# Prompt attention groups combined block by block during the gate projection, on GpSimd, in a hybrid decoder layer

## The chip, the cores and the metric

The kernel runs on one core of one Trainium2 chip. The metric is the device time of one execution in microseconds (us). The engines are TensorE (PE; its weight loads stand in the trace as PEld), VectorE (DVE), ScalarE (ACT), GpSimd (POOL) and SyncE (SP), which here only issues DMAs. A row of the trace gives the start in us from the beginning of the profiled span, the duration in us, the engine, the line of the kernel, the operation and its tiles.

## The reference, cut to what matters

One decoder layer for 1024 prompt tokens and 8 x 8 new tokens ("samples") that share the weights: a half SwiGLU step, a mixer with two branches (an mLSTM and a dilated attention with three head groups), and another half SwiGLU step. What the change touches is the end of the attention branch. Each of the three groups g leaves for each token and head an output and a log of its softmax denominator, and the groups are merged with these as weights:

```
wts = jax.nn.softmax(jnp.stack(lses), axis=0)
y_a = jnp.einsum('gbsh,gbshd->bshd', wts, jnp.stack(outs)).reshape(B, S, A_OUT_WIDTH)
y_a = y_a @ w_up_a
merged = jax.nn.sigmoid(gm) * y_m + jax.nn.sigmoid(ga) * y_a
x = x + merged @ w_out
```

The sample rows attend to cached keys and values (8 sequences with 1152 kept keys each) and to their 8 new keys and values.

## The kernel before, in words

Weights stream as slabs of 128 x 2048 floats (1 MB). Each slab lands in `raw`, and POOL splits it into a high and a low part, one instruction each (`ring_split`, L737 and L739); PE makes three products per tile from the parts. Three slabs are in flight; a slab may be split once PE has released a place.

After the first SwiGLU and the q, k, v projections comes the **slot stage**. Slot n (0 to 83) is half of a projection unit on PE (`pair_unit`, 24 matmuls) followed by a piece of other work (`mixture_slot`). Slots 3 to 39 do prompt attention; each of its 35 units stores unnormalised outputs, their sum and the negated maximum to the DRAM tensor `o_att` (token, group, head, 66 floats). From slot 44 on the mLSTM runs in ten slots for each of four heads (`lstm_slot`, position i = 0 to 9): at slot 44 + 10h + i PE turns and scores chunk i (`keys_and_scores`, L958, L959), DVE scales (L1995), updates the state and the hidden rows. At i = 6 DVE prepares the decay of the next head (`args`, L1958 to L1967), at i = 7 the samples' values (`sample_parts`), at i = 1 it needs a square root from ACT for the previous head (L1530, L2052, L2053). Slots 36 to 83 project the two branch gates, which ACT evacuates with a sigmoid in each odd slot (L1471). Slots 84 to 90 finish the last head without projections.

Then comes the **tail**, in which nothing is projected. SP loads the cached keys `kc` (8 loads) and values `vc` (8 loads); half of them, for pass 0, are issued at slot 82 (`SLOTS - 2`) and behind slot 83. Pass B (B = 0, 1; four sequences each) is: `s_scores` (L1129, L1135 cached keys, L1142 new keys), `s_max` on DVE (L2160), `s_exps` on ACT (L1610), `s_turn` on PE (L1154), a copy on DVE (L2171), `s_values` on PE (L1165, L1167), `s_outputs`, `s_out_turn` (L1174) and `s_out` (L2184), which leaves `soT`. The wait before L1142 is for the semaphore `s_new`, which counts the new keys `sks` and the new values `vnw` together.

Interleaved with the two passes, eight blocks of 128 tokens are combined: SP loads `oc` from `o_att` (two buffers), DVE forms the weights' exponents (L2194 to L2196), ACT takes the exponential (L1616), DVE multiplies and adds (L2203 to L2207), divides (L2209, L2212) into `yat`, PE turns it (`c_turn`, L1183), DVE copies it out (L2220) and SP stores it to `mix[4:6]`. On PE the order is fixed by hand: scores 0, turn of block 0, `s_turn(0)`, block 1, values 0, block 2, `s_out_turn(0)`, blocks 3 to 5, scores 1, turn, values 1, block 6, out turn 1, block 7.

After both, the **merge stage** multiplies the branches with `w_up` (L774 to L776 on `mx_hi`, `mx_lo`), gates them with `sgate` (L2262) and goes on to `w_out`. It needs the inputs `mxin` (six loads from `mix` for each chunk of 384 tokens), the three slabs from `S_UP` on, and the samples' rows stored from `soT`.

Of the kernel before, what the change touches and what calls it, by code (L numbers as in the profile page):

```python
# [116 lines left out]
S_NEW = 16 * (8 + G)  # L117
# [7 lines left out]
HEAD_SLOTS = 10  # L125
SLOTS_END = LSTM_SLOT + HEAD_SLOTS * H + 7
# [3 lines left out]
def program(nc, stream, xT, cols, masks, amasks, cos_t, sin_t, state_in, m_in, kc_in, vc_in,  # L130
# [14 lines left out]
    with ctx:  # L145
# [99 lines left out]
        put = overlay(TEMP + 6144)  # L245
        sqj = put("sqj", [P, DK])
# [38 lines left out]
        ocw = put("ocw", [P, 2, G, H])  # L285
        ocm = put("ocm", [P, 2, H])
# [7 lines left out]
        put = overlay(TEMP + 6656)  # L294
        smk = put("smk", [SROW, KEYS_S])
        put = overlay(TEMP + 6656)
        sqs = put("sqs", [P, G, 2, SAMP])
        yat = put("yat", [P, 2, H * HD])
        yT = put("yT", [P, 2, 2, P])
        put = overlay(ACTS)  # L300
        oc = put("oc", [P, 2, G, H, HD + 2])
        oacc = put("oacc", [P, 2, H, HD + 1])
# [24 lines left out]
        c_in = [sem(f"c_in{i}") for i in range(2)]  # L327
        mix_stored = [sem(f"mix_stored{i}") for i in range(2)]
# [58 lines left out]
        oc_read = sem("oc_read")  # L387
        oce_ready = sem("oce_ready")
# [12 lines left out]
        s_queries = sem("s_queries")  # L401
        s_new = sem("s_new")
# [46 lines left out]
        def _(sp):  # L449
# [119 lines left out]
            def slot(m):  # L569
# [62 lines left out]
            load_heads(sks, kr_out, s_new)  # L632
# [10 lines left out]
            for n in range(2):  # L643
                sp.dma_start(oc[:, n], o_att[n * P:(n + 1) * P]).then_inc(c_in[n], 16)
# [17 lines left out]
            def combined(n):  # L662
                if n + 2 < NBLK:
                    sp.wait_ge(oc_read, n + 1)
                    sp.dma_start(oc[:, n % 2], o_att[(n + 2) * P:(n + 3) * P]).then_inc(c_in[n % 2], 16)
                sp.wait_ge(yT_ready, n + 1)
# [8 lines left out]
            for n in range(2, 5):  # L675
                combined(n)
# [1749 lines left out]
```

## Time and profile before

| | us |
|---|---|
| three timed runs | 2746.63, 2737.41, 2746.70 |
| median | 2746.63 |
| profiled execution, device time | 2736.92 |
| its span | 2734.7 |
| PE busy in the span | 2581.5 (94%) |
| DVE, POOL, ACT busy | 975.4, 816.9, 431.1 |

The profiled execution is a run of its own, near the fastest of the three. PE is busy nearly everywhere; in the page's 40 slices of 68 us the PE digits are 9 except at the start and in slices 24 to 28 (`3 7 8 9 8`), which hold the end of the slot stage, the tail and the merge stage.

### The profile page before, as it was taken

Reading aid. Unit: us, or ns where it says so; the run is one execution under the profiler, and the core shown is the slowest. Engines: PE = TensorE matmul, PEld = TensorE weight load, DVE = VectorE, ACT = ScalarE, POOL = GpSimd, SP = SyncE. Lnnn points to the kernel's source line nnn. Section 1 sums busy time; section 2 is a strip of 40 time slices with the busy share of each in tenths; the row PEclk is TensorE's granted clock in tenths of the full one; section 3 lists DMA queues with packets and bytes.
Section 4 is the critical chain, followed back from the end, with each engine's and each line's share of the span. In section 5 each row is a group of like instructions: output and inputs, shape, how many; then the busy total and the mean of one; then the engine's idle time right before and its main releaser. Section 6 shows DMA issues by size and latency. Waiting matters only on the chain. (4 is left out here: it accounts for less than half of the span.)

```text
span 2734.7 us, 39075 instructions
## 1 busy us (share of the span) xinstructions
PE 2581.5 (94%) x16101; PEld 2513.9 (92%) x16101; DVE 975.4 (36%) x1969; ACT 431.1 (16%) x934; POOL 816.9 (30%) x202
## 2 busy tenths in 40 slices
PE   7999999999998999999999963789899999999997
PEld 6999999999997999989999951789899999999997
DVE  5322222222256134322244335545522222222226
ACT  4100000000031000133433320112200000000003
POOL 3333333333322423322132103041333333333330
PEclk9999999999999999999999986889999999999999
DMA  4110111111102524514333275440111111111101
GB/s 151 56 46 32 46 46 46 46 46 46 46 16 85 175 73 123 140 58 123 109 138 131 101 277 228 150 137 16 45 56 38 46 46 46 46 46 46 37 10 66
DMA packets 102912, 219.72 MB, mean 80 GB/s; under 512 B 30788, under 2 KB 81404, under 8 KB 87836
## 3 DMA queue, kind: packets, MB, share of 16 engines
q1 hardware_dynamic: 61544, 188.80, 20.0%
q10 hardware_dynamic: 41268, 29.50, 3.4%
q8 instruction: 73, 1.20, 0.2%
q14 instruction: 27, 0.22, 0.0%
HBM read 172.38 MB, written 45.89 MB: 80 GB/s over the span
## 5 line engine op out<-in xcount | busy, mean ns | idle before, releaser
L822 PE MATMUL ps<-h_hi,whi 128*128 128x384 f32 (+1 forms) x3072 | 1017.0, 331 | 11.8 <-DVE h_lo L1709 11.8
L823 PE MATMUL ps<-h_lo,whi 128*128 128x384 f32 (+1 forms) x3072 | 1007.5, 328 | 0.0
L824 PE MATMUL ps<-h_hi,wlo 128*128 128x384 f32 (+1 forms) x3072 | 1007.4, 328 | 0.0
L737 POOL TENSOR_TENSOR whi<-raw,con 128x2048 fp32r<-128x2048 f32 x98 | 353.8, 3610 | 1841.9 <-PEq L805 1548.7
L822 PEld LDWEIGHTS ps<-h_hi,whi 128*128 128x128 f32 x3072 | 578.9, 188 | 16.6 <-issue 10.5
L823 PEld LDWEIGHTS ps<-h_lo,whi 128*128 128x128 f32 x3072 | 579.0, 188 | 0.7 <-issue 0.2
L824 PEld LDWEIGHTS ps<-h_hi,wlo 128*128 128x128 f32 x3072 | 578.5, 188 | 0.0
L739 POOL TENSOR_TENSOR wlo<-raw,whi 128x2048 fp32r<-128x2048 f32 x98 | 454.6, 4639 | 7.7
L774 PE MATMUL ps<-act_hi,whi 128*128 128x384 f32 (+1 forms) x1056 | 346.1, 328 | 9.8 <-DVE x L1729 7.7
L1738 DVE TENSOR_TENSOR ps<-silu,ps 128x384 f32<-128x384 f32 x132 | 71.3, 540 | 793.1 <-PE ps L824 555.3
L1729 DVE SCALAR_TENSOR_TENSOR x<-ps,x 128x384 f32<-128x384 f32 (+1 forms) x528 | 281.8, 535 | 201.0 <-PE ps L776 199.5
L776 PE MATMUL ps<-act_hi,wlo 128*128 128x384 f32 (+1 forms) x1056 | 345.5, 327 | 0.0
L775 PE MATMUL ps<-act_lo,whi 128*128 128x384 f32 (+1 forms) x1056 | 345.4, 327 | 0.0
L1300 ACT ACTIVATE silu<-ps 128x384 f32<-128x384 f32 x132 | 62.4, 473 | 1250.5 <-PE ps L824 1250.4
L774 PEld LDWEIGHTS ps<-act_hi,whi 128*128 128x128 f32 x1056 | 198.3, 188 | 12.1 <-DVE x L1729 8.8
L775 PEld LDWEIGHTS ps<-act_lo,whi 128*128 128x128 f32 x1056 | 198.4, 188 | 0.0
L776 PEld LDWEIGHTS ps<-act_hi,wlo 128*128 128x128 f32 x1056 | 198.3, 188 | 0.0
L774 PE MATMUL ps<-whi,h_hi 128*128 128x256 f32 x360 | 103.3, 287 | 7.8 <-DVE h_lo L1709 7.6
L775 PE MATMUL ps<-wlo,h_hi 128*128 128x256 f32 x360 | 102.5, 285 | 0.0
L776 PE MATMUL ps<-whi,h_lo 128*128 128x256 f32 x360 | 102.0, 283 | 0.0
L1740 DVE TENSOR_TENSOR act_lo<-ps,act_hi 128x384 fp32r<-128x384 f32 x132 | 70.7, 536 | 71.2 <-ACT act_hi L1302 71.2
L774 PEld LDWEIGHTS ps<-whi,h_hi 128*128 128x128 f32 x360 | 69.4, 193 | 9.2 <-DVE h_lo L1709 9.2
(226 smaller groups left out, 2094.6 us busy)
## 6 DMA issues: line engine op xcount, KB each, us to landing
raw<-stream SPq DMA_DIRECT2D x99, 1024.0 KB, 4.8
vc<-vc_in SPq DMA_DIRECT2D x8, 1170.0 KB, 11.1
kc<-kc_in SPq DMA_DIRECT2D x8, 1152.0 KB, 9.5
zgate<-stage ACTq DMA_DIRECT2D x16, 384.0 KB, 2.4
sgate<-zgate SPq DMA_DIRECT2D x16, 384.0 KB, 3.3
zqko<-stage ACTq DMA_DIRECT2D x12, 384.0 KB, 2.7
oc<-o_att SPq DMA_DIRECT2D x8, 396.0 KB, 3.9
va_out<-sva ACTq DMA_DIRECT2D x24, 130.0 KB, 1.8
```

The costliest lines, as they stand in the source:

```text
L737: pool.tensor_tensor(hi, raw[:, j, :], con[:, C_ONES:C_ONES + 1].to_broadcast([P, SLAB]), ALU.mult).then_inc(hi_split, 1)
L739: pool.tensor_tensor(lo, raw[:, j, :], hi.bitcast(F32), ALU.subtract).then_inc(slab_ready, 1)
L774: pe.matmul(out, w_hi, x_hi, start=(k == 0), stop=False)
L775: pe.matmul(out, w_hi, x_lo, start=False, stop=False)
L776: last = pe.matmul(out, w_lo, x_hi, start=False, stop=(k == nk - 1))
L822: pe.matmul(out, w_hi, h_hi[:, k, a:a + w], start=(k == 0), stop=False)
L823: pe.matmul(out, w_hi, h_lo[:, k, a:a + w], start=False, stop=False)
L824: mm = pe.matmul(out, w_lo, h_hi[:, k, a:a + w], start=False, stop=(k == KT - 1))
L1300: act.activation(silu[:, par, 0:w], bank(2 * par, w), ACT.Silu).then_inc(silu_done, 1)
L1729: dve.scalar_tensor_tensor(x[:, d, a:a + w], bank(4 + v % ACC, w), 0.5, x[:, d, a:a + w], ALU.mult, ALU.add).then_inc(acc_free, 1)
L1738: dve.tensor_tensor(up, silu[:, par, 0:w], up, ALU.mult).then_inc(mul_done, 1)
L1740: dve.tensor_tensor(act_lo[:, j, a:a + w], up, act_hi[:, j, a:a + w].bitcast(F32), ALU.subtract).then_inc(pair_free, 1)
```

## The change

It moves the combination of the prompt's groups out of the tail into slots 43 to 81, one block every five slots, and takes its products and sums from DVE to POOL. There is one buffer each for `oc`, `yat` and `yT`, and they lie where nothing else is live in those slots. The turn of block n on PE stands in slot `COMBINE_AT[n]` = 46, 51, 56, ..., 81, ahead of that slot's `L958`; the next slot waits for its copy (`yT_ready`). `ring_split` of the last five slabs of the stage is written out by hand on POOL between the blocks. The mask `smk` is loaded at slot 82 and no longer at slot 60, and DVE's `sample_mask` moves from slot 81 to 82. `s_new` is parted: `s_keys` for the new keys, `s_new` for the values, waited for in `s_values`. In the tail, SP loads the merge stage's first four inputs early and the slabs `S_UP + 3` to `+ 5` behind inputs 4 and 5.

```diff
+COMBINE_AT = [LSTM_SLOT + 2 + 5 * n for n in range(NBLK)]
@@ SP, slot(m)
-                if m == 60:
+                if m == COMBINE_AT[0] - 3:
                     for s in range(2):
                         sp.wait_ge(o_stored[s], 16 * len(UNITS[s::2]))
-                    sp.dma_start(smk[:], amasks[0:SROW, A_SAMP:A_N]).then_inc(s_mask, 16)
+                    load_block(0)
+                if m - 1 in COMBINE_AT:
+                    n = COMBINE_AT.index(m - 1)
+                    if n + 1 < NBLK:
+                        sp.wait_ge(ya_ready, n + 1)
+                        load_block(n + 1)
+                    sp.wait_ge(yT_ready, n + 1)
+                    sp.dma_start(mix[4:6, :, n * P:(n + 1) * P].rearrange("j p t -> p j t"), yT[:]).then_inc(mix_stored, 16)
                 if m >= LSTM_SLOT:
                     lstm_slot(m - LSTM_SLOT)
                 if m == SLOTS - 2:
                     sp.wait_ge(head_done, TURNS * (H - 1))
+                    sp.dma_start(smk[:], amasks[0:SROW, A_SAMP:A_N]).then_inc(s_mask, 16)
                     sp.wait_ge(slab_ready, S_UP)
                     load_keys_s(0)
                     load_keys_s(1)
+                    load_heads(sqs, qr, s_queries)
+                    sp.wait_ge(smb_ready, 1)
                     load_values_s(3)
-                    sp.wait_ge(smb_ready, 1)
-                    load_heads(sqs, qr, s_queries)
...
+            sp.wait_ge(mix_stored, 16 * NBLK)
+            for k in range(4):
+                load_branch(0, k)
             sp.wait_ge(sv_full, 1)
             for b in range(GROUP, NB):
                 load_values_s(b)
...
+            load_branch(0, 4)
+            load_branch(0, 5)
             for s in range(S_UP + 3, S_UP + 6):
                 slab_behind(s, s % 3)
@@ POOL
+            def combine(n):
+                pool.wait_ge(oce_ready, n + 1)
+                for g in range(G):
+                    last = pool.tensor_tensor(oc[:, g, :, 0:HD + 1], oc[:, g, :, 0:HD + 1],
+                                              ocw[:, g, :].unsqueeze(2).to_broadcast([P, H, HD + 1]), ALU.mult)
+                last.then_inc(oc_ready, 1)
+                pool.wait_ge(oc_ready, 3 * n + 1)
+                for g in range(1, G):
+                    pool.tensor_tensor(oc[:, 0, :, 0:HD + 1], oc[:, 0, :, 0:HD + 1], oc[:, g, :, 0:HD + 1],
+                                       ALU.add).then_inc(oc_ready, 1)
+                    pool.wait_ge(oc_ready, 3 * n + 1 + g)
+                pool.wait_ge(oc_read, n + 1)
+                if n > 0:
+                    pool.wait_ge(yt_full, n)
+                pool.tensor_tensor(yat[:], oc[:, 0, :, 0:HD], ocm[:].unsqueeze(2).to_broadcast([P, H, HD]),
+                                   ALU.mult).then_inc(ya_ready, 1)
...
+            mixed = (S_F + 6 + 9) // 3
+            order = [(6 * (s - S_F - 6) - 7, s, None) for s in range(3 * mixed, S_UP)]
+            order += [(COMBINE_AT[n] - 1.5, None, n) for n in range(NBLK)]
+            for _, s, n in sorted(order, key=lambda e: e[0]):
+                if n is None:
+                    ring_split(s // 3, s % 3)
+                else:
+                    combine(n)
@@ PE, keys_and_scores
+                m = LSTM_SLOT + HEAD_SLOTS * h + c
+                if m in COMBINE_AT:
+                    c_turn(COMBINE_AT.index(m))
+                elif m - 1 in COMBINE_AT:
+                    pe.wait_ge(yT_ready, COMBINE_AT.index(m - 1) + 1)
@@ PE, tail
-                pe.wait_ge(s_new, S_NEW)
+                pe.wait_ge(s_keys, S_KEYS)
...
-            s_scores(0)
-            c_turn(0)
-            s_turn(0)
-            c_turn(1)
...
+            for B in range(PASSES):
+                s_scores(B)
+                s_turn(B)
+                s_values(B)
+                s_out_turn(B)
@@ ACT, mixture_slot(n)
+                for at_ in (n + 1, n + 2):
+                    if n % 2 == 0 and at_ in COMBINE_AT:
+                        group_exps(COMBINE_AT.index(at_))
@@ DVE
+            def group_weights(n):
+                dve.wait_ge(c_in, 16 * (n + 1))
...
+            def group_sums(n):
+                dve.wait_ge(oc_ready, 3 * n + 3)
+                dve.reciprocal(ocm[:], oc[:, 0, :, HD]).then_inc(oc_read, 1)
...
+                if n in COMBINE_AT:
+                    c_out(COMBINE_AT.index(n))
+                if n + 3 in COMBINE_AT:
+                    group_weights(COMBINE_AT.index(n + 3))
+                if n + 1 in COMBINE_AT:
+                    group_sums(COMBINE_AT.index(n + 1))
-                if n == SLOTS - 3:
+                if n == SLOTS - 2:
                     sample_mask()
```

## Rows read from the trace of the kernel before

**Rows 1.** Waits by pair: in all, times, longest; turns of blocks in the tail.
```profile
PE ps L1183 <- DVE yat L2212: 50.6, 8, 15.8
```
**Rows 2.** Timeline of the tail: start, us, engine, line, tiles, [idle before <- releaser].
```profile
1633.54 0.43 DVE L2206 TENSOR_TENSOR oacc<-oc 128x260 f32<-128x260 f32 x1
...
1641.61 3.71 DVE L2206 TENSOR_TENSOR oacc<-oc 128x260 f32<-128x260 f32 x1
1645.11 4.56 POOL L739 TENSOR_TENSOR wlo<-raw,whi 128x2048 fp32r<-128x2048 f32 x1
...
1653.75 0.69 PE L1183 MATMUL ps<-con,yat 128*128 128x128 f32 x2 [15.76 <-DVE yat L2212]
```
**Rows 3.** Timeline of the tail: both passes' scores, pass 1 to its end.
```profile
1628.10 0.83 PE L1142 MATMUL ps<-sks,sqb 128*32 128x8 f32 x48 [5.09 <-DMA vnw<-va_out]
...
1686.71 5.63 PE L1135 MATMUL ps<-kc,sqb 128*32 128x128 f32 x48
...
1699.80 5.98 PE L1165 MATMUL ps<-vc,spt 128*32 128x260 f32 x72 [1.76 <-DVE spt L2173]
...
1712.36 0.28 DVE L2184 COPY soT<-ps 64x128 f32<-64x128 f32 x1 [0.57 <-PE ps L1174]
```
**Rows 4.** Timeline of DVE: the merge stage's first gating.
```profile
1726.52 0.56 DVE L2262 TENSOR_TENSOR mgt<-ps,sgate 128x384 f32<-128x384 f32 x1 [4.57 <-PE ps L776]
```
**Rows 5.** Timeline of SP's queue: DMA issues, from slot 82 to the end of the tail.
```profile
1589.36 1.28 SPq L604 DMA_DIRECT2D kc<-kc_in  x2
...
1626.92 0.83 SPq L644 DMA_DIRECT2D oc<-o_att  x2
...
1686.59 3.07 SPq L451 DMA_DIRECT2D raw<-stream  x3
```
**Rows 6.** Two stretches: length, busy time (count) of PE, PEld, DVE, ACT, POOL; clock; DMA share; GB/s.
```profile
1590.00:1626.00 36.00, 26.50 (x163) 17.58 (x161) 13.21 (x46) 9.43 (x26) 0.00 (x0) 0.80 0.98 359
1630.00:1650.00 20.00, 2.82 (x12) 2.34 (x12) 15.59 (x26) 1.85 (x5) 8.69 (x3) 0.59 1.01 416
```
**Rows 7.** The tile kc: its loads' time to landing.
```profile
DMA to landing us min/median/max: 6.0/9.5/20.1
```
**Rows 8.** Timeline of slots 43 to 45: SP's queue, PE and DVE.
```profile
1389.68 1.22 SPq L451 DMA_DIRECT2D raw<-stream  x2
...
1395.64 0.27 PE L958 MATMUL ps<-con,kT 128*128 128x128 f32 x1
...
1392.02 0.29 DVE L1995 TENSOR_TENSOR Pm<-ps,Wd 128x128 f32<-128x128 f32 x1 [4.56 <-ACT Wd L1503]
```
**Rows 9.** The tile raw, 1380 to 1402: its three loads' time to landing.
```profile
DMA to landing us min/median/max: 5.0/10.1/12.1
```
**Rows 10.** Timelines of slots 51, 52: a split on POOL, the decay on DVE, the next L958.
```profile
1425.94 6.50 POOL L739 TENSOR_TENSOR wlo<-raw,whi 128x2048 fp32r<-128x2048 f32 x1
...
1427.90 4.63 DVE L1967 SCALAR_TENSOR_TENSOR Wd<-Wd,gcol,msk 64x64 f32<-64x64 f32 x1
...
1432.88 0.27 PE L958 MATMUL ps<-con,kT 128*64 128x128 f32 x1 [2.97 <-DVE Pm L1995]
```
**Rows 11.** Timelines of ACT, DVE and PE, slots 55 and 56 (i = 1, 2).
```profile
1453.93 1.28 ACT L1530 ACT_TABLE_LOAD   x1
1455.22 0.30 ACT L1530 ACTIVATE var<-var,con 128x9 f32<-128x9 f32 x1
...
1455.81 0.17 DVE L2053 TENSOR_TENSOR scl<-var,rden 128x9 f32<-128x9 f32 x1
...
1457.37 0.27 PE L958 MATMUL ps<-con,kT 128*128 128x128 f32 x1
```
**Rows 12.** Timelines of DVE and PE: the end of slot 60's decay, and slot 61; slot 81.
```profile
1483.64 0.28 DVE L1967 SCALAR_TENSOR_TENSOR Wd<-Wd,gcol,msk 64x64 f32<-64x64 f32 x1
...
1484.02 0.27 PE L958 MATMUL ps<-con,kT 128*128 128x128 f32 x1
...
1594.04 1.65 DVE L1984 TENSOR_SCALAR vex<-v,own 64x129 f32<-64x129 f32 x8
```

More of the change, by code:

```diff
@@ L116 @@
 S_QUERIES = 16 * 8
-S_NEW = 16 * (8 + G)
+S_KEYS = 16 * 8
+S_NEW = 16 * G
 ATT_IN = (16 * 8, 16 * 8, 16 * 16)
@@ L245, in program @@
         put = overlay(TEMP + 6144)
+        oc = put("oc", [P, G, H, HD + 2])
+        yat = put("yat", [P, H, HD])
+        yT = put("yT", [P, 2, P])
+        ocw = put("ocw", [P, G, H])
+        ocm = put("ocm", [P, H])
+        put = overlay(TEMP + 11904)
         sqj = put("sqj", [P, DK])
@@ L293, in program @@
         so = put("so", [P, 2, H, HD])
-        put = overlay(TEMP + 6656)
+        put = overlay(X_HI)
         smk = put("smk", [SROW, KEYS_S])
-        put = overlay(TEMP + 6656)
+        put = overlay(TEMP + 8192)
         sqs = put("sqs", [P, G, 2, SAMP])
[L298 to L302, printed above, removed]
         put = overlay(ACTS)
@@ L326, in program @@
         blk_ready = sem("blk_ready")
-        c_in = [sem(f"c_in{i}") for i in range(2)]
-        mix_stored = [sem(f"mix_stored{i}") for i in range(2)]
+        c_in = sem("c_in")
+        mix_stored = sem("mix_stored")
         con_in = sem("con_in")
@@ L749, in _ @@
             ring_split(0, 2)
-            with pool.Fori(1, S_OUT // 3 + 1) as i:
+            mixed = (S_F + 6 + 9) // 3
+            with pool.Fori(1, mixed) as i:
                 for j in range(3):
                     ring_split(i, j)
+            order = [(6 * (s - S_F - 6) - 7, s, None) for s in range(3 * mixed, S_UP)]
[5 more added lines that the diff above has]
+                    combine(n)
+            for s in range(S_UP, S_OUT + 1):
+                ring_split(s // 3, s % 3)
             ring_split(S_OUT // 3 + 1, 0)
@@ L946, in where, with c_turn @@
                 return n, slice(c * P, c * P + n)
+            def c_turn(n):
+                pe.wait_ge(ya_ready, n + 1)
+                if n > 0:
+                    pe.wait_ge(yT_ready, n)
+                for i in range(2):
+                    mm = pe.transpose(ps[:, 5, 256 + i * P:256 + (i + 1) * P],
+                                      yat[:, 2 * i:2 * i + 2, :].rearrange("p h e -> p (h e)"), ident)
+                mm.then_inc(yt_full, 1)
             def keys_and_scores(h, c):
@@ L1175, in s_out_turn @@
                 mm.then_inc(sot_full, 1)
-            def c_turn(n):
-                pe.wait_ge(ya_ready, n + 1)
-                if n >= 1:
-                    pe.wait_ge(yT_ready, n)
-                for i in range(2):
-                    mm = pe.transpose(ps[:, 7, i * P:(i + 1) * P], yat[:, n % 2, i * P:(i + 1) * P], ident)
-                mm.then_inc(yt_full, 1)
-            s_scores(0)
-            c_turn(0)
-            s_turn(0)
-            c_turn(1)
-            s_values(0)
-            c_turn(2)
-            s_out_turn(0)
-            for n in range(3, 6):
-                c_turn(n)
-            s_scores(1)
-            s_turn(1)
-            s_values(1)
-            c_turn(6)
-            s_out_turn(1)
-            c_turn(7)
+            for B in range(PASSES):
[3 more added lines that the diff above has]
+                s_out_turn(B)
             pe.wait_ge(slab_ready, S_UP + 3)
@@ L1495, in att_copy, with group_exps @@
                 act.activation(apt[u % 2][:], ps[:, 6, :], ACT.Copy).then_inc(pt_ready, 1)
+            def group_exps(n):
+                act.wait_ge(ocw_ready, n + 1)
+                act.activation(ocw[:], ocw[:], ACT.Exp).then_inc(oce_ready, 1)
             def exps(h):
@@ L1612, in s_exps @@
                 ins.then_inc(sp_ready, 1)
-            def group_exps(n):
-                act.wait_ge(ocw_ready, n + 1)
-                act.activation(ocw[:, n % 2], ocw[:, n % 2], ACT.Exp).then_inc(oce_ready, 1)
             s_exps(0)
-            for n in range(6):
-                group_exps(n)
             s_exps(1)
-            for n in range(6, NBLK):
-                group_exps(n)
-            act.wait_ge(ya_ready, NBLK)
             for k in range(6):
@@ L2232, in _ @@
             s_outputs(0)
-            block(2)
             s_out(0)
-            for n in range(3, 6):
-                block(n)
             s_max(1)
@@ L2239, in _ @@
             s_outputs(1)
-            block(6)
             s_out(1)
-            block(7)
             def branch_low(c, k):
```

86 lines of the change are left out of this document (20 added, 66 removed).

## The prediction

> **What bounds the kernel now.** I read the page's 40 slices first: PE is the engine that is always busy, but for slices 24 to 28. Then the waits by pair: in the tail PE waits 50.6 us, eight times, for `yat` [rows 1], the block that DVE has just combined and that PE's fixed order wants turned before it goes on. The timeline of the tail shows the worst one, 15.76 us, with `s_values(0)` standing behind it [rows 2]. Its cause is in the same rows: the sum of 0.43 us takes 3.71 us when POOL is splitting a slab, and ends when POOL's instruction does. So from about 1616 to 1722 PE is not the bound; a chain is (scores, maxima, exponentials, turn, values, and eight blocks in between), ending with `soT` at 1712.64 [rows 3] and the first gating of the merge stage at 1726.52 [rows 4]. Whatever shortens the chain shortens the kernel one for one, until a transfer ends later. Before slot 84 it is the other way round: PE is the bound, DVE has 3 to 4 us free in each slot of about 5.3 us, and what is added there costs only where PE comes to wait. The sum is therefore tail gain minus slot stalls, against the profiled execution's 2736.92 us. That one lies 9.7 under the median of the timed runs, 2746.63; with it, two of four runs lie near 2737 and two near 2747, so I count the result from their middle, 2742.
>
> **The tail, part by part.**
> 1. Scores 0 no longer wait for the values: 5.09 us [rows 3]. The new keys are issued ahead of three 1.2 MB value loads and the `vnw` loads behind them, so I take them as landed. Scores 0 end at 1628.93 - 5.1 = 1623.8.
> 2. Pass 0 without blocks. Pass 1 gives the durations: from the first key matmul to `s_values` 1699.80 - 1686.71 = 13.1 us [rows 3], and from there 5.98 + about 0.6 for the new values, 0.7 for DVE's division, 1.1 for the out turn, 0.3 for the copy: 8.9 us. So 22.0 us from first key matmul to `soT`. Pass 0 would be over near 1640, and pass 1 could start there instead of at 1686.71.
> 3. It can't, since now transfers end last. The DMA engines are full from 1590 to 1626 (share 0.98) and again from 1630 to 1650 (1.01, 416 GB/s) [rows 6]. Keys 6 and 7 are issued behind `sample_scored`, and the slowest key load takes 20.1 us [rows 7], so they land near 1652. What changes for them: three `oc` loads of 0.4 MB go from in front of them [rows 5], 1.2 MB / 0.416 = 2.9 us less. But SP now reaches slot 82's loads later. It must first store block 7, which DVE copies behind `sample_parts` of slot 81, over at 1595.7 [rows 12], plus 0.6: SP goes on at 1596.5, and issues the first keys near 1597 and not at 1589.36 [rows 5]. 7.7 us of full rate are lost, of which the dips of the first stretch (359 against 416 [rows 6]: 36 x 57 / 416 = 4.9 us) can give back up to 4.9; bounds 2.8 to 7.7, I take 4.5. The store of head 3 lands behind this backlog, and keys 4 and 5 wait for it as the `oc` loads do at 1626.92 [rows 5]: 1631.4. From there 7.9 MB (four key loads, three slabs) at 0.41 MB per us are 19.2 us, with a little of the merge inputs: pass 1 starts at 1651.5, and `soT` would come at 1673.5. The four values (4.8 MB, with 0.8 MB merge inputs) land by about 1665, wanted at 1664.6: 0.5 more. `soT` at 1674.
> 4. Slabs 59 to 61 are split on POOL in 3 x 8.4 = 25 us from about 1643, ready at 1668: covered by the chain by 6 us. If they landed 12 us later they would be the bound.
> 5. From `soT` to the first gating: before 1726.52 - 1712.64 = 13.9 us, two blocks' work among them. Now SP has behind `soT` inputs 4 and 5 (which wait for DVE's `mx_lo`, 1.1 us), then three slabs of 1 MB that before were issued at 1686.59 [rows 5], then the four `soT` stores, and `sgate` behind their landing. 3.1 MB at 0.416 take 7.6 us, and the stores land behind them: 1.7 + 7.6 + about 0.7 + 3.2 for `sgate` = 13.2 us. The blocks' time is given back to the slabs. Bounds: 8 (stores not held by slabs) to 16.
> Gain of the tail: 1712.64 - 1674 + 0.7 = **39.3 us**. With pass 1 at 1640 in place of 1651.5 (point 3) it would be 51.
>
> **The slot stage, part by part.**
> 1. Block 0. DVE's `group_weights(0)` stands in slot 43 and waits for a load that SP issues right behind slab 55, at 1390.2 [rows 8]. That slab lands 10.1 us after 1389.7 [rows 9], so `oc` at about 1400.3, where DVE was ready at 1387.5 (its next instruction idled 4.56 us [rows 8]). Queued behind the wait on ACT are `group_exps(0)` and the exponentials of head 0's decay, and behind those on DVE the masked scores of slot 44, at 1392.02 before [rows 8]. They come at about 1402.7; PE wants them at 1395.64 [rows 8]: 7.0 us. Bounds: 1 (landing in 4) to 9.5 (12.1).
> 2. POOL's instructions. No row has a small one. 2048 elements take 4.56 us [rows 2], 2.23 ns each, so 260 take 0.58 if the time goes by the elements. The bounds are DVE's 0.43 and, if it were all fixed cost, the split's 4.56 [rows 2]; I take 0.58, since the instruction on DVE shrinks in this way too, and leave the far end to rival C. The first five of a block run a slot ahead, hidden; the last (`yat`) is on the path: DVE's reciprocal, product, three handovers, 1.1 us from DVE's last instruction before it to PE.
> 3. Slots at i = 7 behind a decay (51, 61, 71). At slot 61 the decay ends at 1483.92 and PE wants L958 at 1484.02 [rows 12]: 1.0 us. The other two by like rows 0.9 and 1.6: 3.5.
> 4. Slots at i = 2 behind a head's square root (56, 66, 76). The exponential of the block needs another table on ACT, and the sigmoid's back again, ahead of the root: 1.28 us per load [rows 11]. DVE's `scl` ends at 1455.98, plus 1.28 + 1.1, against L958 at 1457.37 [rows 11]: 1.0. The others by like rows 1.0 and 1.7: 3.7.
> 5. POOL and DVE in each other's way. In slot 51 the split and the decay collide: 4.63 us for an instruction of 0.28, and PE waits 2.97 [rows 10]. After the change POOL holds that split back until block 1 is over, so this collision goes, but the split then falls on `sample_parts` and the copy of the turned block, for which slot 52 now waits. I count this place as even, and the same at slots 71 and 72 (new) as 1.5; bounds 0 to 4 each.
> 6. Sixteen turns on PE: 0.3 us per block beside 0.69 in the tail [rows 2]: 2.4.
> Sum: 7.0 + 3.5 + 3.7 + 1.5 + 2.4 = **18.1 us**. `s_scores` start, mask (0.15 MB, DVE idle in slot 83) and the 16 extra table loads in other slots are covered by 3 us of idle time per slot; if that cover is gone, each table load is 1.3 us.
>
> The collision is what the Trainium skill describes (SBUF: State Buffer, on the port pair shared by DVE and GpSimd): an exclusive lock, the later one blocks fully. By that rule the trace agrees, and every new POOL product is a chance of a block. For a table switch the skill (ScalarE: Activation LUTs, What ACT_TABLE_LOAD costs) gives 1283 ns plus a drain of 1380 ns; the next instruction here starts at 1455.22, 1.29 after the load began [rows 11], so no drain is seen; with it, three i = 2 slots would cost an estimated 4 us more.
>
> **The rivals.**
> A. *Covered slots.* Block 0's load is early, and DVE's and POOL's lateness is absorbed: slots cost 5. 39.3 - 5 = 34 us gained, 2708. For it: 3 us idle per slot; against: the order behind slab 55.
> B. *The tail is held by transfers longer.* The backlog of slot 82 costs its full 7.7, pass 1's values land 5 late, and slabs sit in front of the stores for 16: 39.3 - 3.2 - 5 - 2.8 = 28, minus 18.1: 10 gained, 2732. For it: share 1.01.
> C. *Slower: the blocks' handover chain stalls every slot.* Each block goes DVE, ACT, POOL, DVE, POOL, PE, DVE, PE. If locks, a fixed cost of POOL's products and table loads make PE wait more than 39.3 / 8 = 4.9 us per block, the kernel is slower; at 6.5 us per block, 52 - 39.3 = 13 lost, 2755. Against: only one lock of over 3 us reaches PE in the slots before (2.97).
> D. *The change doesn't do what it says:* the new keys land no earlier than the values did. Then 5.1 of the gain is nothing on PE; as transfers bound pass 1, the time moves by 1 at most: 2722. It is within the forecast.
> By the skill (GPSIMD Engine Reference, Engine selection) two-input elementwise work is about twice as slow on GpSimd. That rule holds for the work moved, and its time is off the path but for `yat`; by it `yat` would take an estimated 0.9 us, 2 us more in all, no other result.
>
> **How the numbers follow.** Forecast: 39.3 - 18.1 = 21.2 us gained, 2742 - 21 = 2721 us (2715.7 against the profiled execution), chance 0.52 with D, own range 2708 to 2732. A 0.18, B 0.19, C 0.11. The range takes in A with its lower level of run (2737 - 37 = 2700) and B with the upper (2747 - 7 = 2740). Half a per cent, 13.7 us, is about what a measurement tells from no change. Faster by more: the forecast but for its weak end, and A: 0.72. Within: B mostly: 0.19. Slower: 0.09.
>
> **What would show it.** Right: PE's wait at slot 45 of about 7 us for `Pm`; waits of 1 to 2 us ahead of `L958` or the turn at slots 51, 56, 61, 66, 71, 76; first `kc` load near slot 82's L958; in the tail a PE wait for DMA `kc` of about 10 us ahead of pass 1's L1135, no waits for `yat`; `soT` 39 us nearer to the first `L1129`-run's start than the old 97 us; first `sgate` landing 13 us behind `soT`. Wrong: a POOL product of over 1 us (the reading by elements falls), or a wait at the merge stage's start for slab 61.

## The result, and the profile after

| | before | after |
|---|---|---|
| timed runs, median (lowest to highest) | 2745.57 us (2737.41 to 2747.55), 6 runs | 2725.47 us (2725.15 to 2727.34), 6 runs |
| profiled execution: its time, and its span | 2736.92, 2734.7 | 2727.34, 2725.3 |
| slot 44's key turn to slot 82's, on PE | 205.5 us | 233.0 us |
| slot 82's key turn to the end of `soT` | 116.1 us | 80.3 us |
| end of `soT` to the first gating on DVE | 13.9 us | 17.5 us |

The ratio is 0.9945, 95% interval 0.9928 to 0.9961: faster, by 11 to 20 us. The forecast was 2721 us, the range 2700 to 2740. The two profiled executions differ by less, 9.6 us; the section on the prediction comes back to this. One of the four timed runs of e10 below was a slow one, at 5112.67 us, and is left out of its median.

A slot's key turn is its L958, the turn of its keys. The lines have moved: L958 is now L997, L1135 is L1174, L1165 is L1205, L2184 is L2231, L1984 is L2002, and POOL's split L737 and L739 is L732 and L734. First the page of after, its slices (each a fortieth of the span, busy tenths):

```profile
PE   7999999999997999999988895789999999999997
DVE  5322222222246134422225431546522222222226
PEclk9999999999998999999999996889999999999999
DMA  3111111111102523524333338540011111111101
```

Counted from 0, slices 23 to 28 of PE's row were `6 3 7 8 9 8` before and are `9 5 7 8 9 9` now: the hole is shallower and begins later, and it is still there. New are the three digits 8 in slices 20 to 22 (1363 to 1567 us, in the slot stage), which were 9. PE's waits by pair (in all, times, longest) say what is in it and what came new:

```profile
PE ps L1174 <- DMA kc<-kc_in: 11.4, 2, 10.1
PE ps L997 <- DVE yT L2126: 9.1, 2, 4.9
PE ps L997 <- ACT kw L1539: 7.6, 1, 7.6
PE ps L978 <- POOL yat L756: 5.9, 6, 1.5
```

The 50.6 us for combined blocks in the tail [rows 1] have gone. In their place stand 11.4 us for keys from DMA (tail) and 22.6 us in three new groups of the slot stage: for the copy of a turned block, for block 0's exponentials (`kw` on ACT) and for POOL's product `yat`. The timeline of the tail, which answers to [rows 3] and [rows 4], PE and then DVE:

```profile
1662.60 6.38 PE L1205 MATMUL ps<-vc,spt 128*32 128x260 f32 x72 [1.76 <-DVE spt L2220]
...
1681.66 5.31 PE L1174 MATMUL ps<-kc,sqb 128*32 128x128 f32 x48 [10.06 <-DMA kc<-kc_in]
...
1696.40 6.54 PE L1205 MATMUL ps<-vc,spt 128*32 128x260 f32 x72 [3.43 <-issue]
...
1709.99 0.66 PE L798 MATMUL ps<-mx_hi,whi 128*128 128x384 f32 x1 [5.02 <-DVE mx_lo L2248]
```
```profile
1705.01 0.28 DVE L2231 COPY soT<-ps 64x128 f32<-64x128 f32 x1 [0.74 <-PE ps L1214]
...
1722.78 0.56 DVE L2261 TENSOR_TENSOR mgt<-ps,sgate 128x384 f32<-128x384 f32 x1 [13.04 <-DMA sgate<-zgate]
```

The two longest waits of this tail are for transfers: pass 1 waits 10.06 us for its keys, and the first gating 13.04 us for `sgate`. SP's queue shows why. It answers to [rows 5]:

```profile
1624.57 0.37 SPq L601 DMA_DIRECT2D mix<-yT  x1
...
1625.49 0.90 SPq L619 DMA_DIRECT2D kc<-kc_in  x2
...
1660.55 0.83 SPq L619 DMA_DIRECT2D kc<-kc_in  x2
...
1706.63 1.38 SPq L455 DMA_DIRECT2D raw<-stream  x3
1708.06 3.43 SPq L687 DMA_DIRECT2D mix<-soT  x4
1719.45 4.74 SPq L698 DMA_DIRECT2D sgate<-zgate  x3
```

Block 7's store stands ahead of the first keys, keys 4 and 5 come 35 us behind these, and the 3 MB of slabs go out 1.4 us ahead of the `soT` stores, whose landing `sgate` awaits: 11.4 us from the first store's issue to the first `sgate`.

In the slot stage the rows of block 0 are these, on DVE and on PE, at slot 45. SP issued the load at 1391.31, and DVE could start on it 10.4 us later:

```profile
1401.73 0.17 DVE L2109 TENSOR_TENSOR ocm<-oc 128x4 f32<-128x4 f32 x1 [13.23 <-DMA oc<-o_att]
...
1404.39 0.45 PE L997 MATMUL ps<-con,kT 128*128 128x128 f32 x1 [7.56 <-ACT kw L1539]
```

And these are slots 51 and 52, POOL, DVE and PE, which answer to [rows 10]:

```profile
1435.63 0.61 POOL L756 TENSOR_TENSOR yat<-oc,ocm 128x256 f32<-128x256 f32 x1 [3.38 <-issue]
1436.20 3.60 POOL L732 TENSOR_TENSOR whi<-raw,con 128x2048 fp32r<-128x2048 f32 x1
1439.88 4.54 POOL L734 TENSOR_TENSOR wlo<-raw,whi 128x2048 fp32r<-128x2048 f32 x1
```
```profile
1435.33 0.17 DVE L2119 RECIPROCAL ocm<-oc 128x4 f32<-128x4 f32 x1
...
1438.54 1.28 DVE L2000 TENSOR_SCALAR own<-msk,wsc 64x8 f32<-64x8 f32 x1
1439.86 6.01 DVE L2002 TENSOR_SCALAR vex<-v,own 64x129 f32<-64x129 f32 x8
1445.79 0.41 DVE L2126 COPY yT<-ps 128x256 f32<-128x256 f32 x1
```
```profile
1436.49 0.41 PE L978 MATMUL ps<-con,yat 128*128 128x128 f32 x2 [0.63 <-POOL yat L756]
...
1446.34 0.40 PE L997 MATMUL ps<-con,kT 128*64 128x128 f32 x1 [4.91 <-DVE yT L2126]
```

The eight products of L2002 take 1.65 us where they are alone [rows 12, the same instructions before]; here they take 6.01. The longest of them takes 4.64 us, about as long as POOL's split beside it, which ends at 1439.88 + 4.54 = 1444.42; the other seven follow at 0.27 each. The copy of the turned block stands behind them on DVE, and PE, which the program lets go on only behind this copy (`yT_ready`), stands 4.91 us.

### The profile page after: what moved, and what is told of

It reads as the page before. It is cut to its first block and busy times, and to the rows that moved or that the text cites. A ratio compares the mean times of both kernels' runs of the same rounds, so it can differ in the third digit from the quotient of the medians.

```text
span 2725.3 us, 39068 instructions
## 1 busy us (share of the span) xinstructions
PE 2580.9 (95%) x16101; PEld 2513.9 (92%) x16101; DVE 944.7 (35%) x1921; ACT 448.4 (16%) x948; POOL 845.4 (31%) x250
## 5 line engine op out<-in xcount | busy, mean ns | idle before, releaser
L848 PE MATMUL ps<-h_hi,wlo 128*128 128x384 f32 (+1 forms) x3072 | 1008.3, 328 | 0.0
L732 POOL TENSOR_TENSOR whi<-raw,con 128x2048 fp32r<-128x2048 f32 x98 | 353.5, 3608 | 1637.4 <-PEq L829 1436.7
L734 POOL TENSOR_TENSOR wlo<-raw,whi 128x2048 fp32r<-128x2048 f32 x98 | 452.5, 4618 | 7.7
```

What stands on the lines that cost most here:

```text
L732: pool.tensor_tensor(hi, raw[:, j, :], con[:, C_ONES:C_ONES + 1].to_broadcast([P, SLAB]), ALU.mult).then_inc(hi_split, 1)
L734: pool.tensor_tensor(lo, raw[:, j, :], hi.bitcast(F32), ALU.subtract).then_inc(slab_ready, 1)
L848: mm = pe.matmul(out, w_lo, h_hi[:, k, a:a + w], start=False, stop=(k == KT - 1))
```

## The experiments

All are timed beside the kernel before, whose median lay between 2736.4 and 2742.9 us in these comparisons. They were made at four later times, on different chips (e1 to e4, e5 to e8, e9 and e10, e11), and after was not timed again in them. So a difference between two medians of the table can hold a few us that are not the edit's. By their ratios to before, e3 and e6 (0.9945 and 0.995) can't be told from after (0.9945), and the intervals of e1 (0.9896 to 0.9944), e2 (0.9906 to 0.9945) and e4 (0.9864 to 0.9938) overlap that of after; e5 (0.9978 to 1.0007) and e8 (0.9803 to 0.9853) lie clear of it. What each single edit did is therefore read from its trace. To place a gain I use PE's key turns of slots 44 and 82, the end of `soT` and the first product of the merge stage, in each run's trace:

| run | median us | slots 44 to 82 | slot 82 to start of `soT`'s last copy | slot 82 to merge stage | merge stage to end |
|---|---|---|---|---|---|
| before | 2745.57 | 205.5 | 115.8 | 125.7 | 1012.5 |
| after | 2725.47 | 233.0 | 80.0 | 85.0 | 1015.3 |
| e1 block 0 early | 2716.03 | 222.5 | 79.5 | 84.5 | 1015.4 |
| e2 slabs ahead | 2720.76 | 232.4 | 79.8 | 84.9 | 1008.8 |
| e3 keys ahead | 2722.48 | 232.8 | 76.5 | 81.6 | 1015.5 |
| e4 split behind | 2712.23 | 218.9 | 80.0 | 85.0 | 1015.9 |
| e5 on DVE | 2738.01 | 245.0 | 78.2 | 83.3 | 1014.4 |
| e6 scores wait | 2726.25 | 231.9 | 80.4 | 85.4 | 1015.6 |
| e7 keys alone, in before | 2733.68 | 205.6 | 114.7 | 124.6 | 1006.5 |
| e8 all four | 2693.22 | 209.5 | 75.7 | 80.8 | 1008.4 |
| e9 keys 4, 5 early | 2689.24 | 209.6 | 73.7 | 78.8 | 1010.8 |
| e10 keys 6, 7 first | 2688.61 | 209.6 | 73.6 | 79.4 | 1005.1 |
| e11 reciprocal first | 2684.90 | 207.1 | 74.5 | 79.7 | 1008.3 |

In e9 and e11 the row of slot 82's key turn is missing from the trace and in e9 that of slot 44; their places are taken from the rows beside them. The last column varies by 5.7 us between runs that share their code from there on (e2 and e8 to e11), and by 6.0 between before and e7: a difference of a few us in a median alone is not read as an effect here.

### e1: block 0's rows loaded earlier

```diff
                 if u == last_of[2]:
+                    for s in range(2):
+                        sp.wait_ge(o_stored[s], 16 * len(UNITS[s::2]))
+                    load_block(0)
                     sp.wait_ge(gcol_ready, 1)
...
-                if m == COMBINE_AT[0] - 3:
-                    for s in range(2):
-                        sp.wait_ge(o_stored[s], 16 * len(UNITS[s::2]))
-                    load_block(0)
```

> The changed kernel, with block 0's load issued at slot 39, right behind the last attention store and ahead of head 1's loads and slab 55, in place of slot 43. Theory (the wait of 7.6 us at slot 45 is the queue in front of this one load): the wait goes, and with it 1.5 us of slow clock behind it in slot 46; 9 us less than the changed kernel, 2716. Rival (the first block's chain DVE, ACT, POOL itself is slow, or the load is only displaced onto head 1's loads, which then come late for their own users): 0 to 2 us less.

Measured: 2716.03 us (2715.06 to 2720.24), 9.4 less than after. The wait for `kw` is gone; key turns of slots 44 to 46:

```profile
1391.27 0.27 PE L996 MATMUL ps<-con,kT 128*128 128x128 f32 x1
1395.85 0.27 PE L996 MATMUL ps<-con,kT 128*128 128x128 f32 x1
1400.38 0.27 PE L996 MATMUL ps<-con,kT 128*128 128x128 f32 x1
```

The stage is 10.4 us shorter, though the wait was 7.6. Of this, 9.3 us lie between the key turns of slots 44 and 46 (18.4 us in after, 9.1 here). The 1.7 us beyond the wait are clock: the stretch behind the wait, in after and then in e1 (length, busy us of PE, PEld, DVE, ACT, POOL, then the granted clock, DMA share, GB/s):

```profile
1404.00:1409.00 5.00, 4.61 (x23) 4.64 (x24) 1.21 (x5) 2.83 (x5) 4.19 (x5) 0.63 0.34 103
```
```profile
1404.00:1409.00 5.00, 5.00 (x35) 4.99 (x34) 1.32 (x5) 1.48 (x5) 2.22 (x1) 1.00 0.83 279
```

In the same 5 us PE did 23 matmuls at a granted clock of 0.63, where it did 35 at 1.00. Cut finer, the clock of after is 0.50 up to 1406.5 (the lower level, 1.2 GHz), 0.75 in the mean of the next 2.5 us and 1.00 (2.4 GHz) from 1409. Half of the 2.1 busy us up to 1406.5 and a quarter of the 2.5 behind are 1.7 us. The last 1.1 us of the 10.4 lie further on; 0.7 of them are in slots 52 to 54, where PE has the same wait of 4.9 us in both runs. This wait on PE is paid for twice.

### e2: the three slabs ahead of the merge inputs

```diff
-            load_branch(0, 4)
-            load_branch(0, 5)
             for s in range(S_UP + 3, S_UP + 6):
                 slab_behind(s, s % 3)
+            load_branch(0, 4)
+            load_branch(0, 5)
             sp.wait_ge(soT_ready, PASSES)
```

> The changed kernel, with the three slabs from S_UP + 3 issued ahead of merge inputs 4 and 5, as before the change, so that nothing large stands in front of the stores of soT. Theory (the gap from soT to the first gating, 17.5 us, holds about 9 us of slab transfer): the gap falls to about 9 us, 8.5 us less, 2717. Rival (the slabs, now wanted while the values of pass 1 land, delay those values by as much): soT comes later by 5 to 8 us and the time stays at 2723 to 2725.

Measured: 2720.76 us (2715.2 to 2724.52), 4.7 less; its span is 6.4 less. SP's queue and DVE's first gating:

```profile
1679.63 16.65 SPq L455 DMA_DIRECT2D raw<-stream  x3
...
1706.65 2.39 SPq L687 DMA_DIRECT2D mix<-soT  x4
1710.32 6.24 SPq L698 DMA_DIRECT2D sgate<-zgate  x3
```
```profile
1714.39 0.56 DVE L2261 TENSOR_TENSOR mgt<-ps,sgate 128x384 f32<-128x384 f32 x1 [4.54 <-PE ps L800]
```

`sgate` follows the stores by 3.7 us and not 11.4, and gating now waits for PE. It comes 8.4 us earlier; 6.4 of these reach the end. The rival falls: `soT` ends 80.1 us behind slot 82's turn, as in after (80.3).

### e3: the first keys ahead of block 7's store

```diff
+                if m == SLOTS - 2:
+                    sp.wait_ge(head_done, TURNS * (H - 1))
+                    sp.dma_start(smk[:], amasks[0:SROW, A_SAMP:A_N]).then_inc(s_mask, 16)
+                    sp.wait_ge(slab_ready, S_UP)
+                    load_keys_s(0)
+                    load_keys_s(1)
                 if m - 1 in COMBINE_AT:
                     n = COMBINE_AT.index(m - 1)
```

(with the same five lines taken out of their place behind the store)

> The changed kernel, with the mask and the first two cached keys of slot 82 issued ahead of the wait for block 7's turned copy and not behind it. Theory (from slot 82 on the tail is bound by transfers, and SP came to them 7.9 us late): first keys issued near 1617.5 and not at 1625.5, pass 1's key matmuls 5 to 8 us earlier, 5 to 8 us less, 2718 to 2720. Rival (the order of transfers decides, not their start: keys 6 and 7 wait for head 3's store and its wait): under 2 us less.

Measured: 2722.48 us (2719.66 to 2728.09), 3.0 less. The two medians alone can't show this, since the times of after lie inside this range; the trace shows 3.4 us in the tail and 2.7 in the span, between the theory and its rival. The first keys are issued 7 us earlier, the third pair only 3:

```profile
1618.55 1.36 SPq L620 DMA_DIRECT2D kc<-kc_in  x2
...
1657.68 0.83 SPq L620 DMA_DIRECT2D kc<-kc_in  x2
```

So the lateness of the first keys, which I had charged with 4.5 us, is worth the 3.4 us by which the tail got shorter. The loads of keys 4 and 5 stand behind the wait for head 3's stores as well.

### e4: the two splits behind the copy of the turned block

```diff
                 if n is None:
+                    if s in (S_UP - 4, S_UP - 1):
+                        pool.wait_ge(yT_ready, 2 if s == S_UP - 4 else 6)
                     ring_split(s // 3, s % 3)
```

> The changed kernel, with POOL waiting for the copy of the turned block (yT_ready) before it splits slabs 55 and 58, so that the splits do not fall on sample_parts and the copy of slots 51 and 71. Theory (the waits of 4.9 and 4.2 us at slots 52 and 72 are the port lock): both go, and with them 3 us of slow clock behind them; 9.4 us less, 2716. Rival (DVE is simply late there, its work of slots 51 and 71 being too long): 0 to 2 us less. Second rival: the splits now fall on DVE's work of the next slots and the waits move there: 2 to 5 us less.

Measured: 2712.23 us (2711.57 to 2713.14), 13.2 less. DVE's products in slot 52 are back at their own time, and POOL's split comes behind them:

```profile
1437.80 0.21 DVE L2002 TENSOR_SCALAR own<-msk,wsc 64x8 f32<-64x8 f32 x1
1438.05 1.65 DVE L2004 TENSOR_SCALAR vex<-v,own 64x129 f32<-64x129 f32 x8
...
1440.11 3.60 POOL L732 TENSOR_TENSOR whi<-raw,con 128x2048 fp32r<-128x2048 f32 x1 [4.61 <-DVE yT L2128]
```

The two waits were 9.1 us and are gone, so both rivals fall; the stage is 14.0 us shorter. From the key turn of slot 51 to that of slot 54 after takes 25.5 us and e4 17.9, which is 7.6 for a wait of 4.91; from slot 71 to 74 it is 25.8 against 19.2, 6.5 for a wait of 4.21. In after the clock behind the first of them is at its lower level again, with PE busy:

```profile
1446.00:1450.00 4.00, 3.66 (x15) 3.35 (x16) 1.40 (x5) 0.56 (x3) 0.00 (x0) 0.50 0.65 193
1450.00:1454.00 4.00, 4.00 (x22) 3.75 (x20) 0.00 (x0) 0.53 (x1) 0.00 (x0) 0.74 0.32 123
1454.00:1458.00 4.00, 4.00 (x25) 2.82 (x23) 1.78 (x7) 3.21 (x6) 0.00 (x0) 1.00 0.22 82
```

In e4 it is 1.00 from 1438 to 1462. Half of the 3.66 busy us and a quarter of the next 4 are 2.9 us, about the 2.7 that the first place cost beyond its wait. No slab came late: PE's only wait for a split, 8.4 us, stands in after too.

### e5: products and sums on DVE

```diff
                 dve.wait_ge(oce_ready, n + 1)
+                for g in range(G):
+                    last = dve.tensor_tensor(oc[:, g, :, 0:HD + 1], ... ocw[:, g, :] ..., ALU.mult)
+                for g in range(1, G):
+                    dve.tensor_tensor(oc[:, 0, :, 0:HD + 1], ... oc[:, g, :, 0:HD + 1], ALU.add)
                 dve.reciprocal(ocm[:], oc[:, 0, :, HD])
+                dve.tensor_tensor(yat[:], oc[:, 0, :, 0:HD], ... ocm[:] ..., ALU.mult)
```

(and `combine` taken out on POOL)

> The changed kernel with one thing different: the products, sums and the combined rows of a block are made by VectorE at the same place of the order (end of the slot before the block closes) and GpSimd combines nothing. Theory (an operation on VectorE costs its time on the chain that TensorE waits for, and GpSimd's own splits go on beside it): some 11 to 15 us of VectorE work more over eight blocks at slots that TensorE follows closely, so 2735 to 2745 us against 2725 of the changed kernel. Rival (GpSimd's slower operations and its handovers of 0.6 to 1.5 us a block cost as much as VectorE would): within 3 us of 2725.

Measured: 2738.01 us (2735.01 to 2741.22): 12.5 more than after, and even with before (ratio 0.9993, 0.9978 to 1.0007). With these operations on DVE in this place nothing is left of the gain. PE's wait for the combined rows:

```profile
PE ps L957 <- DVE yat L2111: 24.2, 6, 9.8
```

instead of 5.9 us in after, where 9.1 us stood for the copy besides, which are gone here. DVE's six large operations of a block take about 2.4 us together (1.10, 0.86 and 0.42), but DVE is the engine PE follows in these slots, and in slot 50 the two sums met a split and took 5.07 us for their 0.86, behind a small operation of the decay (L1960) that had met the same split's first instruction and took 3.39 for 0.15. That is a wait of 9.83 out of the 24.2. The edit does a little more than it says: with no block on POOL, that slab's split begins at 1434.67 and is no longer held behind block 1. So part of the 12.5 us may be the split's new place; what DVE would cost with the split held back was not run.

### e6: the scores wait for the new values again

```diff
                 pe.wait_ge(s_keys, S_KEYS)
+                pe.wait_ge(s_new, S_NEW)
```

> The changed kernel with one thing different: the scores wait again for the new values as well as for the new keys. Theory: in the changed kernel the last keys of the pass (issued at 1660.55 us behind head 3's store) are what the scores wait for in the end, and the new values are long there by then, so 0 to 1 us more than 2725. Rival: the scores of the first pass begin late by the time of the first value products, some 5 us, and pass it on to the end: 2730 us.

Measured: 2726.25 us (2724.86 to 2726.83), 0.8 more. The end is as the theory had it, for a reason it did not have. PE in the tail:

```profile
1660.58 0.83 PE L1182 MATMUL ps<-sks,sqb 128*32 128x8 f32 x48 [7.13 <-DMA vnw<-va_out]
...
1681.89 6.20 PE L1174 MATMUL ps<-kc,sqb 128*32 128x128 f32 x48 [4.39 <-DMA kc<-kc_in]
```

The values are *not* long there: the scores stand 7.13 us for them. But pass 1 then waits 4.39 for its keys, not 10.06, and starts at 1681.89 where it was 1681.66. Counted from slot 82's turn it starts 1.9 us later, has a shorter wait ahead of its values, 2.0 us for 3.4, and `soT` ends 0.4 us later (80.6, 80.3). The new semaphore gains at most that in this kernel; the transfers set pass 1.

### e7: the split of the wait alone, in the kernel before

```diff
-                pe.wait_ge(s_new, S_NEW)
+                pe.wait_ge(s_keys, S_KEYS)
```

(with the key rows counted on `s_keys`, and the wait for `s_new` set ahead of the new values' products)

> The kernel before with one part of the change alone: the scores wait for the new keys and not for the new values; groups are combined in the tail as before. Theory (as in the prediction: scores of the first pass stood 5.09 us for the values): 3 to 5 us less than before, a ratio of 0.998 to 0.999. Rival (the pass is set by its transfers, and what the scores gain they wait later): no difference, within 1 us.

Measured: 2733.68 us (2729.73 to 2740.99, 12 runs) against 2740.67, ratio 0.998 (0.9967 to 0.9993): 2 to 9 us less. Its trace supports less. PE no longer waits ahead of the new keys' scores, but then

```profile
1634.05 0.69 PE L1186 MATMUL ps<-con,yat 128*128 128x128 f32 x2 [10.64 <-DVE yat L2215]
```

where before it had this:

```profile
1635.17 0.69 PE L1183 MATMUL ps<-con,yat 128*128 128x128 f32 x2 [6.24 <-DVE yat L2212]
```

The waits for blocks are 55.4 us in all, not 50.6 [rows 1], and the merge stage starts 1.1 us earlier (1721.14, 1722.23). Of the 7.1 us between the two spans, 6.0 lie behind the merge stage's start, where both run the same code. They are mostly clock: over the first 80 us of that stage it is 0.88 in before and 0.94 here, and 0.06 of 80 us are 4.8. The clearest place is one matmul, released by `mx_lo` behind a wait of 3.2 or 3.3 us in before, in e7 and in after alike. These are 6 us from it on, one line each for before, e7 and after:

```profile
1755.00:1761.00 6.00, 5.57 (x17) 5.58 (x18) 0.93 (x2) 0.00 (x0) 0.00 (x0) 0.50 0.13 49
1751.00:1757.00 6.00, 5.50 (x23) 5.51 (x24) 1.58 (x4) 0.00 (x0) 0.00 (x0) 0.72 0.14 53
1750.00:1756.00 6.00, 5.44 (x31) 5.44 (x32) 2.46 (x6) 0.49 (x1) 0.00 (x0) 1.00 0.20 58
```

Behind equal waits PE did 17, 23 and 31 matmuls, at a clock of 0.50, 0.72 and 1.00. So this difference is no effect of e7's edit, and what decides it no run here shows.

### e8 to e11: the four edits together, and three more steps

e8 is after with the edits of e1 to e4.

> The changed kernel with the four edits tried one by one together: block 0's rows loaded earlier, the gate slabs ahead of the branch's loads, the first keys ahead of block 7's store wait, and the two splits behind the transposed rows. Theory (they act at different places, so their gains of 9.4, 4.7, 3.0 and 13.2 us add): about 2695 us. Rival (the earlier slots only bring the tail's transfers forward into each other, so that slabs, keys and stores take back what the slots gain): 2703 us or more.

Measured: 2693.22 us (2689.49 to 2694.85), ratio to before 0.983. They add, within the few us that such sums can be trusted to: 30.3 us by their own runs, 32.3 together. Slots 44 to 82 now take 4.0 us more than before the change, not 27.5.

e9 issues keys 4 and 5 ahead of the waits for head 3's stores:

```diff
+            for b in range(GROUP, 6):
+                load_keys_s(b)
             units_stored(60)
             sp.wait_ge(hidden_stored, 16 * H)
```

> The four edits together (2693 us) and one more: keys 4 and 5 of the second pass are issued right behind the new values' rows, ahead of the waits for the head's stores. Theory (in the run of the four together the transfers are busy for 0.90 of the stretch before 1640 us and all of it behind, and the second pass waits 10.28 us for its keys): the 2 us of idle transfers are filled and the end comes some 2 to 3 us earlier, about 2690.5. Rival (keys 6 and 7 stand behind three slabs anyway and set the wait): no difference, within 1 us of 2693.

Measured: 2689.24 us (2685.64 to 2690.83), 4.0 less than e8, which the ranges and ratios (0.9817, 0.9828) do not set apart; in the traces the tail is 2.0 us shorter and the span 1.9, the theory's size.

e10 puts keys 6 and 7 ahead of the three slabs as well:

```diff
             sp.wait_ge(sample_scored, 1)
+            for b in range(6, NB):
+                load_keys_s(b)
             for s in range(S_UP, S_UP + 3):
                 slab_behind(s, s % 3)
```

> The kernel of the run named before this one, and keys 6 and 7 issued ahead of the three slabs of 1 MB each that stood before them. Theory (the second pass waits for the last keys, and 3 MB at some 420 GB/s ahead of them are 7 us; the slabs have slack, since GpSimd needs 25 us for the three and the gating products that read them begin 30 us later): the wait of 10.28 us falls to some 3 us and the end comes 4 to 7 us earlier, about 2685. Rival (the values and the next slabs queue behind the slabs just the same, so that the second pass waits for its values, or the gating products wait for their slabs): within 2 us of the run before, or slower.

Measured: 2688.61 us (2687.36 to 2691.55, three runs), no difference. The wait has moved, as its rival said. Keys, and the values of pass 1:

```profile
1645.73 5.76 PE L1176 MATMUL ps<-kc,sqb 128*32 128x128 f32 x48 [2.35 <-DMA kc<-kc_in]
...
1666.71 5.58 PE L1207 MATMUL ps<-vc,spt 128*32 128x260 f32 x72 [9.66 <-issue]
```

For the second the profile names no releaser; the four value loads were issued from 1641.38 on and took 19.4 us to land in the median, which fits. In e9 the two waits were 9.73 and 2.16 us, in all as much. With keys, values and slabs wanted at once, this order decided only which of them was waited for.

e11 is e9 with DVE's reciprocal ahead of its other work of the slot, for blocks 1 to 6:

```diff
+                if n + 1 in COMBINE_AT[2::2]:
+                    group_sums(COMBINE_AT.index(n + 1))
                 if n >= LSTM_SLOT:
                     lstm_slot(n - LSTM_SLOT)
```

(and for the other three inside `args`, ahead of the mask products)

> The kernel with the four edits and keys 4 and 5 early (2689 us), and one more: in the six slots before blocks 1 to 6 close, VectorE takes the reciprocal of the summed denominators ahead of its other work of the slot (in every second of them ahead of the 2.2 us of mask products), not as the slot's last instruction; GpSimd had the sums ready 3 to 8 us before. Theory (the six waits of TensorE for the combined rows, 5.9 us in all, are this place in VectorE's order and no speed of GpSimd): the six waits go and the end comes 4 to 6 us earlier, about 2684.5. Rival (TensorE's chain with VectorE and ScalarE in the slot is due then anyway, and another wait stands in the same place): within 1.5 us of 2689.

Measured: 2684.90 us (2680.56 to 2689.44), 4.3 less than e9 and 0.979 of before (0.9777 to 0.9808); the interval overlaps that of e9 (0.9794 to 0.9841), and the two spans differ by 1.5 us. The six waits for `yat`, 5.9 us, are all gone. The stage is only 2.5 us shorter, since PE's wait for a head's normalised rows takes some of it back, 2.06 us at slot 66:

```profile
1511.62 0.53 PE L1054 MATMUL ps<-con,hn 128*128 128x128 f32 x2 [2.06 <-ACT hn L1562]
```

e11 has the lowest median of all, 40.6 us under that of the changed kernel, with the same operations; against e9 the gain is not clear of the noise.

## Why the prediction came true, and where its sum did not

The mechanism was right: the blocks leave the tail, PE pays for them in the slots, transfers set pass 1, and the gain is the difference. The number, 4.5 us off, is better than the sum behind it, and that is luck. From trace to trace the first gating should have come 21.2 us earlier, and came 3.7 earlier (1722.78 against 1726.52). The terms of the missing 17.5:

1. *Slots, 27.5 us against 18.1.* The terms of which I had rows were close. Block 0: 7.72 (slot 45's turn behind slot 44's, less e1's 4.58) for 7.0. The waits ahead of the turn at i = 7: 0.63, 0.83, 1.46 for 0.9, 1.0, 1.6. At i = 2: 0.74, 0.78, 1.46 for 1.0, 1.0, 1.7. POOL's product: 0.62 us and sum 0.74 for 0.58; `yat` 0.61, 1.5 times DVE's 0.42, so the estimate of 0.9 by a factor of two was too high. The step that failed is 5, POOL and DVE in each other's way. I had counted slots 51 and 52 even and 71 and 72 at 1.5, and left the collision with `sample_parts`, which I had named, at that. It cost waits of 4.9 at slot 52 and 4.2 at slot 72, and e4 shows that with the slow stretches behind both it was 14.0 us. Before had a wait of its own at slot 52, the 2.97 of [rows 10], and took 22.6 us from slot 51's key turn to slot 54's against 17.9 in e4. So against before the two places cost 2.9 and 6.5 us, where even and 1.5 were forecast: 7.9 of the 9.4 us missing here. The bounds of 0 to 4 held for the first and not for the second.
2. *The clock behind a wait stood in no term.* At their places the waits of 7.6, 4.9 and 4.2 us were worth 9.3, 7.6 and 6.5. The rows of before showed a clock of 0.80 and 0.59 where PE waited [rows 6], and the prediction makes nothing of it. This is part of the 9.4 us, not a term beside it.
3. *Step 3 of the tail.* `soT` ended 80.3 us behind slot 82's key turn, forecast 77.5. The wait for keys, "about 10 us", measured 10.06. SP's lateness was there: the first keys came 0.45 us behind slot 82's turn, and e3 prices it at 3.4, against 4.5 taken. A pass, forecast 22.0, took 23.6 with a wait of 3.43 ahead of its values instead of 1.76.
4. *Step 5 of the tail, 17.5 us against 13.2,* just outside the bounds of 8 to 16. Slabs ahead of the stores is what I had described, but `sgate` was held 11.4 us by the stores' landing, not 8.3. e2 removes it: 9.1 us from `soT` to the gating.
5. *Slot 44 came 1.0 us later.* This is no effect: in after and e2 to e6, which share their code up to there, slot 44's key turn lies anywhere from 1391.3 to 1392.9.

Sum: 9.4 + 2.8 + 4.3 + 1.0 = 17.5. Of it 5.7 came back later: from the first gating to the end after takes 1002.5 us, before 1008.2. That after had begun its merge products 12.2 us earlier doesn't explain this: e7 had begun them 1.1 us earlier, runs before's code there, and takes 1002.7. The clock rows shown with e7 explain 2.8 us of it at their one place (half of the 5.57 busy us at 0.50 in before, nothing in after); this part is one of the execution and not of the change. So the profiled executions differ by 9.6 us, less than half of the 21.2 that the sum had forecast for them.

The timed medians differ by 20 and their ratio gives 15. All six timed runs of after lie within 2.2 us, while those of before spread over 10 (and over 18 in all comparisons, 2729 to 2747). I had put the level of before at 2742, above its profile, and this, with the 5.7 us that came back, made the number right; neither is a term of the sum. The two levels that I saw in four runs of before are not there in more: 60 later ones fill the range from 2729 to 2747 and above 2731.5 leave no gap of 1 us. Their granted clock goes with the time, from 0.972 in the fastest to 0.968 in the slowest, and 0.004 of 2740 us are 11 of the 18 us. Why the clock differs, and why the runs of after differ less, stays open.

*Step 1 of the tail,* the 5.09 us for the scores, was no gain: e6 has the wait back at 7.13 us at no cost, and e7 has it gone from before with 4.4 us of it back in the next wait. *The signs:* the wait at slot 45 came as forecast in size, for `kw` on ACT and not for `Pm` on DVE; no POOL product took over 1 us. *The rivals:* A (covered slots) falls: 27.5 us, not 5. B's 2732 was not reached, though slabs in front of the stores cost more than it said. C is right in kind (the locks reach PE at blocks 1 and 5 with 4.9 and 4.2 us) and wrong in the mean, 27.5 / 8 = 3.4 us per block against the 4.9 from which it decides. D falls: in after the scores have no wait for the new keys, where e6 has one of 7.13 for the values.

The Trainium skill (SBUF — State Buffer, on the port pair shared by DVE and GpSimd) describes the lock; slot 52 and e4 agree, at 6.01 us against 1.65. Its drain of 1380 ns behind a table load (ScalarE: Activation LUTs, What ACT_TABLE_LOAD costs) would have made the three waits at i = 2 longer than I forecast; they were shorter, 2.98 us in all, so no such term is seen here.

## What to carry to other kernels

Work moved off a chain that waits into a stage that doesn't is paid for where it meets the other engine's long instruction; before moving it, look at what else of that stage stands within a few us of the new place, and make the one that has slack wait (here a slab split, two waits for 13 us). Price a new wait on TensorE with the slow stretch behind it, here 1.7, 2.7 and 2.3 us on top of waits of 7.6, 4.9 and 4.2. And where transfers are the bound, ask of every freed wait what is waited for next: here one run added a wait of 7 us and another took one of 7 away, and neither moved the end.

## What was unexpected of the hardware

A product by one column on DVE (L2002, from `v` to `vex`, no PSUM operand) is held by POOL's split as a sum of two tensors is: 6.01 us against 1.65, and 1.28 us for one of 0.21. Behind a wait of 4.9 us PE ran at the lower level, 0.50, for 4 us and more though it was busy (3.66 of the 4 us from 1446), and behind one of 7.6 us as well; what e1 and e4 gained at these places beyond the waits is this. A wait of 3.2 us at one place of the merge stage was followed by 6 us at 0.50 in before, and one of 3.3 us at the same place in after by none. Products of 260 elements take 0.62 us on POOL and those of 2048 take 3.60, so, if the two forms are alike, a small one has a fixed part of about 0.2 us: (3.60 - 0.62) / 1788 is 1.67 ns an element, and 260 of these are 0.43.
